# Sharing the page loads of a decoder's sequence stage between two queues

## What is computed

```python
k_past = cache_sb_k[l][page_table].reshape(db, past_len, C_HEADS, HEAD_DIM)
v_past = cache_sb_v[l][page_table].reshape(db, past_len, C_HEADS, HEAD_DIM)
...
z = jnp.einsum('bqhd,bkhd->bhqk', q, k).astype(jnp.float32) * (q.shape[-1] ** -0.5)
log_keep = jnp.where(strict, jax.nn.log_sigmoid(-z), 0.0)
after = lax.cumsum(log_keep, axis=3, reverse=True) - log_keep
a = jnp.where(strict, jnp.exp(jax.nn.log_sigmoid(z) + after), 0.0)
```

## Time and profile before

| | us |
|---|---|
| median of 3 runs | 2253.36 |
| lowest and highest | 2248.74, 2261.6 |
| the profiled execution | 2257.88 |
| its span, first to last instruction | 2256.1 |
| of it PE busy | 1912.2 (85%) |
| sequence stage, layer 0 (page scores of b = 0 to those of b = 7) | 352.33 to 489.97 |
| mean granted clock of PE, as a share of full speed | 0.895 |

### The profile page before, as it was taken

One profiled execution on the slowest core, in us unless ns is written; L12 is line 12 of the kernel. 1 busy time (PEld: TensorE's weight loads), 2 busy tenths in 40 slices (PEclk: granted clock), 3 DMA queues, 4 the chain that ended last, 5 costly groups with the idle time before them and its releaser, 6 DMA issues. The chain is left out here.

```text
span 2256.1 us, 24189 instructions
## 1 busy us (share of the span) xinstructions
PE 1912.2 (85%) x9680; PEld 984.3 (44%) x9680; DVE 560.5 (25%) x1256; ACT 368.7 (16%) x681; POOL 35.8 (2%) x59
## 2 busy tenths in 40 slices
PE   5896566779899999999969955577879999999995
PEld 2474453336434444444436634334543444444442
DVE  0121445553101111111033125455330111111103
ACT  1121013332101101100122200243110110110011
POOL 0001100000000000000000001000000000000000
PEclk9898558889889999999989955699878999999998
DMA  9624007985969999999952310489416999999992
GB/s 400 277 96 157 12 14 263 329 304 212 393 279 403 380 377 379 372 405 377 380 225 75 106 72 15 171 303 348 178 56 279 400 381 383 373 374 402 379 380 100
DMA packets 111865, 609.75 MB, mean 270 GB/s; under 512 B 13220, under 2 KB 15525, under 8 KB 49923
## 3 DMA queue, kind: packets, MB, share of 16 engines
q1 hardware_dynamic: 108690, 595.77, 66.8%
q0 software_dynamic: 3056, 12.35, 1.7%
HBM read 602.26 MB, written 5.81 MB: 270 GB/s over the span
## 5 line engine op out<-in xcount | busy, mean ns | idle before, releaser
L978 PE MATMUL PS<-ring,big 128*64 128x512 f32 x3072 | 682.1, 599 | 6.7 <-ACT big L1121 6.0
L978 PEld LDWEIGHTS PS<-ring,big 128*64 128x64 f32 x3072 | 215.0, 138 | 428.5 <-issue 419.6
L1121 ACT ACTIVATE big<-PS 128x512 f32<-128x512 f32 (+9 forms) x202 | 145.5, 731 | 1144.0 <-PE PS L978 394.0
L1451 DVE TENSOR_TENSOR big<-big,PS 128x320 f32<-128x320 f32 (+5 forms) x180 | 96.3, 542 | 743.3 <-PE PS L957 428.7
L945 PE MATMUL PS<-big 128*128 128x256 f32 (+1 forms) x768 | 238.7, 442 | 3.0 <-DVE big L1896 2.3
L597 PE MATMUL PS<-mT,ring 128*128 128x320 f32 x768 | 208.1, 433 | 0.0
L945 PEld LDWEIGHTS PS<-big 128*128 128x128 f32 (+1 forms) x768 | 135.2, 203 | 102.7 <-issue 90.9
L597 PEld LDWEIGHTS PS<-mT,ring 128*128 128x128 f32 x768 | 145.6, 190 | 62.1 <-issue 1.9
L957 PE MATMUL PS<-big 128*128 128x320 f32 x512 | 145.8, 438 | 2.2 <-ACT big L1121 2.2
L957 PEld LDWEIGHTS PS<-big 128*128 128x128 f32 x512 | 94.8, 190 | 62.5 <-issue 22.7
L530 PE MATMUL PS<-cst,big 128*128 128x128 f32 (+5 forms) x490 | 83.8, 299 | 36.2 <-DVE big L1644 26.4
(11 more groups left out here) (275 smaller groups left out, 1303.3 us busy)
## 6 DMA issues: line engine op xcount, KB each, us to landing
ring<-in_w_gate SPq DMA_DIRECT2D x128, 1024.0 KB, 9.6
ring<-in_w_up SPq DMA_DIRECT2D x128, 1024.0 KB, 8.7
ring<-in_w_down SPq DMA_DIRECT2D x128, 1024.0 KB, 7.8
ring<-in_pool_kv SPq DMA_DIRECT2D x256, 256.0 KB, 8.5
ring<-in_w_ada SPq DMA_DIRECT2D x48, 1024.0 KB, 13.5
big<-in_windows SPq DMA_DIRECT2D x16, 2432.0 KB, 8.4
ring<-in_w_in SPq DMA_DIRECT2D x24, 1024.0 KB, 11.8
ring<-in_w_out SPq DMA_DIRECT2D x8, 1024.0 KB, 10.1
```

The source lines that it names most:

```text
L978: i = mm(PS[SLOTS * x:SLOTS * x + SLOTS, out_bank + half, :], stationary(k, x), w, start=(k == 0), stop=(k == steps - 1))
L1121: return nc.scalar.activation(out, in_, ACT.Copy)
L1451: return V.tensor_tensor(out, a, b, op)
```

## The change

For sequences 2 to 7 the sync engine reads the numbers of the even pages only and issues those 8 DMAs. The odd pages are read and issued by ACT: in step b, for b from 1 to 6, between `unit_exp` and the wait for `c_exponents`, ACT reads the 8 odd page numbers of sequence b + 1 into its registers, waits for `c_rows_mm` of sequence b - 1, and issues 8 page DMAs on its own queue. Both count on the same semaphore. Sequences 0 and 1 are loaded as before.

```diff
             def page_numbers(b):
-                return [sp.value_load(page_ids[0:1, PAGES * b + j:PAGES * b + j + 1], min_val=0, max_val=N_POOL - 1) for j in range(PAGES)]
+                return [(j, sp.value_load(page_ids[0:1, PAGES * b + j:PAGES * b + j + 1], min_val=0, max_val=N_POOL - 1))
+                        for j in range(0, PAGES, 2 if b >= 2 else 1)]
...
-                for j, page in enumerate(numbers):
+                for j, page in numbers:
...
+            def odd_pages(l, b):
+
+                numbers = [(j, act.value_load(page_ids[0:1, PAGES * b + j:PAGES * b + j + 1], min_val=0, max_val=N_POOL - 1))
+                           for j in range(1, PAGES, 2)]
+                act.wait_ge(sem["c_rows_mm"], DB * l + b - 1)
+                for j, page in numbers:
+                    src = pool_kv[l, bass.ds(page, 1)].rearrange("a p n -> p (a n)")
+                    act.dma_start(seq.pages[b % 2][:, j, :], src).then_inc(pages_full[b % 2], 16)
+
             def seq_step(l, b, more):
...
                 unit_exp(l, b)
+                if 1 <= b < DB - 1:
+                    odd_pages(l, b + 1)
                 act.wait_ge(sem["c_exponents"], n8)
```

## The result

The changed kernel takes 2307.5 us (median of 4 runs, 2304.5 to 2317.2) against 2256.2 before, a ratio of 1.0231 with an interval of 1.0191 to 1.0272: 51 us slower. The forecast was 2295 in a range of 2262 to 2330. In the code of after, the lines of PE and ACT in this stage stand one later than before (L767 is now L768), the numbers are read at L1299 and the odd pages issued at L1304.

The account below looks back on a forecast made before the run. The sync engine's own instruction stream was taken to set the step. Twelve steps at 286.8 against 241.4 us (+45.4) and the last steps (-3.4) sum to +42 us; against the 2253.4 median that gives 2295 us, range 2262 to 2330.

Parts of the forecast that it names:

- What bounded the kernel before: Sequence stages, steps 1 to 6: the sync engine's stream of reads and issues, 20.2 us, sets the step.
- rival 1: Faster: ACT's work hides, steps fall to the DMA floor of 17.7 us, -30 us, 2223; chance 0.10.
- The block: ACT, mid-step: 8 page numbers at 0.57 us and 8 issues at 0.55 us add 9.0 us.
- Cover, one for one: ACT's idle time ahead of the page weights' Exp hides 2.4 us (b below 4) or 2.8 (b from 4).
- Given back: Behind the block, PE's wait for `unit_weights` and an Exp-to-transposes gap go: 0.8 us for b below 4, 0.4 above.
- PE's clock: After 6 us idle, PE runs slow: 1.4 us for L870's products plus 0.2 for transposes, 1.6 a step.
- Step 7: No block there; it begins with its pages present and PE warm: 1.7 us less twice, -3.4.
- Do the pages come in time: Odd pages, mid-step: all landed at 20 to 22 us, needed at 24, two us to spare.
- The sum: Twelve steps at a mean of 23.9 us: 286.8 against 241.4, +45.4; with step 7's -3.4, +42 us.
- Much slower: ACT's issues stall or its page numbers cost more, block about 12 us: +78 us, 2331; chance 0.11.

Follow-up runs that it names:

- the kernel with double reads: Changed kernel with windows issued only after the previous sequence's pages have landed, and ACT reading its 8 page numbers twice: 2348.6 us, ratio 1.0417.
- windows behind the pages: Changed kernel with one more sync-engine wait: from sequence 3 on, a window is issued only when the previous sequence's 16 pages have landed: 2303.3 us, ratio 1.0203.
- the kernel with 7 filling matmuls: Changed kernel with windows held back until the pages have landed, plus 7 unread matmuls before PE's wait for page weights: 2284.3 us, ratio 1.0117.
- half a block: Changed kernel with ACT reading and issuing only every fourth page, and windows held back until the pages have landed: 2261.9 us, ratio 1.0029.
- the run with GpSimd: Kernel before, with odd pages read and issued by GpSimd under a semaphore of their own, ACT unchanged: 2225.3 us, ratio 0.9872.
- the kernel with reads at the head: Changed kernel with ACT reading its 8 page numbers at the head of the step and only issuing in the middle: 2318.9 us, ratio 1.0224.

## Why the prediction was right

*What bounded the kernel before.* Right. Its stream was the limit, and taking either half of it or the reads away gives 207 us for the twelve steps; the forecast for rival 1, a relief that costs nothing, was 211.

*The block.* 9.0 us forecast, 8.7 measured. The number cost 0.53 us from start to start, less than the 0.57 taken, and the issue 0.50 as a rule, below the lower bound of 0.52 that I had given it, but 0.56 in the mean with its stalls, where I took 0.55.

*Cover, one for one.* Right: 2.4 us of cover stayed (404.68 to 413.05 is the block of 8.3 and no more), and the three block lengths show the slope.

*Given back.* Right for b below 4, with 0.8 us forecast. The transposes of step 2 before, in PE's timeline:

```profile
398.51 0.74 PE L530 MATMUL PS<-cst,big 128*128 128x128 f32 x5
```

From the start of the Exp to that of the transposes it took 1.25 us before (397.26 to 398.51) and 0.82 after (413.05 to 413.87), 0.43 less, and the 0.42 ahead of the unit's turn went too. It doesn't show from the Exp to the products (2.84 us before, 397.26 to 400.10, and 3.00 after, 413.05 to 416.05), since the transposes between them took 0.59 more at the low clock; that belongs to the next term.

*PE's clock.* The mechanism was right, the term too small: this is the term of the sum that was mis-sized. I had 1.6 us for a step, behind 6 us of idling; PE idled 3.8 to 6.9 us ahead of the transposes. In step 2 the products cost 1.71 more, the transposes 0.59 and L873 0.20; in step 1 L873 cost 0.44 more and the turn 0.24; and in two steps of layer 1 the page scores behind them still took 3.64 in place of 1.92. That is 2.1 to 3.2 us in ten steps, 3.7 and 4.9 in the other two, and 2.8 in the mean. Step 2 adds up with it: 17.0 + 8.4 - 2.4 - 0.9 + 2.5 is 24.6, and it took 24.5. It is why b below 4 came to 25.7 us where 24.4 were forecast, in spite of the shorter block; b from 4 came to 23.7 where 23.4 were.

*Step 7.* 1.7 us less each were forecast, 0.5 came: the page scores did run at full speed, but behind ACT's and DVE's short pauses the fold, the transposes (1.31 us for 0.74) and all of the products then ran at the low clock.

*Do the pages come in time.* Too kind: 20 to 22 us forecast, 23.2 to 24.2 measured in the ten steps that issue a window too, with 0.9 us to spare in step 2, nothing in two steps, and not two us. The step that failed was to count the window's and the pages' bytes together at full rate from 8 us on; the pages began only behind the whole of the window's large pieces. In the changed kernel this cost next to nothing (7 us of the sum), but it spoiled every cheaper version. The remark that a step could not fall much below 20 to 21 us with odd pages begun in mid-step held in the mean and not step by step: with windows held back and the eight issues begun 8.3 and 9.0 us into the step, two steps took 18.99 and 18.80 us.

*The sum.* 286.8 forecast, 296.4 measured, and 3.7 more in the steps 0, which the change doesn't touch. There the products took 3.64 us in both layers, before 1.93. In the kernel with double reads, whose step 0 is instruction by instruction that of "windows behind the pages", step 0 took 17.3 us against 18.9, so the same instructions can take either time as the clock's low stretches happen to fall. Of the 17.3 us between forecast and measurement in the profiled executions (2299.9 against 2317.2) 9.6 lie in the twelve steps, 3.7 in the steps 0, 2.4 in the steps 7 and 1.6 elsewhere. By the medians, 2295 against 2307.5, it is 12.5: the profiled execution lay 10 us above its kernel's median, and which of its stretches were the longer ones isn't known.

As an account of the loss: the sync engine's relief is worth 34 us (241 to 207); ACT's block costs about 50 (six steps of 20.7 and six of 22.0 us, as the three clean steps of the kernel with 7 filling matmuls took them, make 257, against 207 without a block); PE's clock about 32 (257 to 289); the order of transfers 7. Less 34, plus 50, 32 and 7 are the 55 measured. The second and third of these rest on three clean steps and are the least certain; the lines of the changed kernel, with 2.8 us a step for the clock, come to 34 for it and so speak for them.

The rivals: "faster" would have needed a block of under 3 us; half a block, of 4.4, gave 1.003. Much slower did not come, since issues on ACT stalled rarely and shortly. Of the Trainium skill's rule (page "Trainium Kernel Development and Optimization", section Key Constraints) that issuing from several engines only saves the sequencer's issue time, the run with GpSimd gives the good side, 31 us, and the changed kernel what the rule leaves open: the time is saved on one sequencer and spent on another, and it is a gain only where nothing stands in line behind it.

## What to carry to other kernels

Before moving DMA issues and register reads to another engine, find what stands behind them on that engine and on whose path it lies: 16 small instructions were 8.7 us there, all but the 2.4 to 2.8 us of idle time at that place on the chain, while an engine with nothing to do took them for free. A queue that is relieved does not only stop being late, it also starts the next transfers earlier, and these can get ahead of transfers that are needed sooner; the order that a slow queue enforced by itself must then be written down. Where a pause of some us is put into PE's chain, its low clock behind the pause has to be priced for everything up to the end of the step, not for the longest group alone.

## What the runs showed of the hardware

A small transfer can stand behind a large one of another queue. A page of 256 KB issued on ACT's queue at 390.22 us, 0.35 ahead of a 2.4 MB window on the sync engine's, landed after 11.9 us, beyond the window's main part, while the three pages just ahead of it landed in 3.0 to 3.7; in the changed kernel pages issued 4.4 us behind a window landed only once its main part had. The trace's DMA packets say where the time went. The window's main part is 128 packets of 19 KB, which take about 0.75 us each, and a page is 128 packets of 2 KB. Of the 512 of ACT's four pages 487 had begun by 394.0 us; the last 25 began one by one up to 400.8, while the window's ran. In the changed kernel none of ACT's began before 412.54, when the last large packet of the window (412.33) had begun. The Trainium skill, page "DMA: Bandwidth & Descriptors", section "Queues, rings and completion order", has each engine take turns between its queues packet by packet, a packet there being a run of typically 9 to 17 descriptors. By that rule size in bytes gives no precedence: a page isn't through sooner for being nine times smaller, and a turn could hold all eight large pieces that a DMA engine has of a window (128 by 16, an estimate). Neither observation speaks against that, but the trace doesn't show how long a turn is, so the cause stays open.

A register read and a DMA issue cost ACT's sequencer what they cost the sync engine's (275 against 267 ns, 340 against 333), and neither waits for an ACTIVATE that is still running: in the changed kernel the first read of step 2 started with the ACTIVATE at 404.68, which took 0.63 us, and in the kernel with reads at the head the first issue at 381.17 lay within one from 381.01 to 381.64.

PE's clock can fall without a single long pause. In the kernel with half a block and windows behind, the pauses ahead of transposes and products were 1.64 and 0.72 us, and the products took 3.43 us; in step 7 of the kernel before they took 3.31 behind a wait of 0.84, and there a wait of 1.70 us was followed by page scores of 3.07 us (step 4) where one of 1.83 was followed by 1.92 (step 6). Which steps it hits changed from kernel to kernel where the instructions were the same, and one mean price for it is no more than a mean.
